# Every main product of a two-block transformer layer reads its moving operand and writes its results from the last column to the first

## The chip, the cores and the metric

The kernel runs on one core of one Trainium2 chip. The metric is device time in microseconds of one execution; the median of three runs of the kernel before is 2672.72 us (2672.32 to 2673.97).

## The reference, cut to what matters

Two transformer blocks run one after the other on a sequence of 256 positions with a model width of 2048, all in float32. Nearly all arithmetic lies in products of an activation with a weight matrix:

```python
# first block
mod = (c @ w_ada + b_ada)                      # modulation, c is one vector
h = rmsnorm(x, g_pre_mix) * (1 + scale1) + shift1
proj = h @ w_in                                # 2048 -> 9472
y_a = sliding_window_attention(...) @ w_attn_proj
y_h = (rmsnorm(hgrn2_recurrence(...)) * sigmoid(g_h)) @ w_hgrn_proj
merged = sigmoid(gate_a) * y_a + sigmoid(gate_h) * y_h
x = x + gate1 * rmsnorm(merged @ w_out, g_post_mix)
gu = h2 @ w_ffn_in                             # 2048 -> 2 x 5632
x = x + gate2 * rmsnorm((silu(g) * u) @ w_ffn_out, g_post_ffn)
# second block
proj = rms_norm(x) @ w_in_2                    # 2048 -> 4096
x = x + concat(moba_attention(q, k, v), multiscale_pool(p)) @ w_out_2
x = x + conv_ffn(rms_norm(x), w_up, conv_w, conv_b, w_down)   # 2048 -> 2 x 5632 -> 2048
```

## The kernel before

Activations lie transposed in SBUF: features on the 128 partitions, the 256 positions (`S`) along the free axis. A product with a weight matrix keeps a 128x128 piece of the weights still in TensorE and moves the activation past it; the result has output features on partitions and positions along the free axis of PSUM.

To keep float32 accuracy with TensorE's one-pass format (fp32r), every operand is split in two, a rounded part (hi) and the remainder (lo). An activation tile such as `X`, `hid`, `merged`, `attn_x` or `hgrn_x` holds for each of its 128-row blocks 512 columns: the 256 hi columns, then the 256 lo columns. For the weights, ScalarE writes `w_hi` from the raw weights (L664) and VectorE writes `w_lo` as the difference (L1174). Each 128x128 piece of weights then takes two matrix instructions, a *pair* below: `w_hi` against all 512 columns, and `w_lo` against the first 256. Both add into one PSUM bank of `psg`, 512 float32 columns wide. When a group has been summed over its contraction, ScalarE copies columns 256 to 511 to `half` (L649) and VectorE adds columns 0 to 255 to it (L1138).

The weights come in 512 KB chunks (four blocks of the contraction by 256 output columns), loaded by the SP queue into a ring of four buffers `raw`. There are 836 chunks, in twenty jobs that run one after the other (the list `jobs`, from `kv` to `dn2b`). TensorE's function `job` goes through the chunks in order: it waits for the chunk's `w_lo` (semaphore `raw_used`), issues 4 x 2 pairs, and signals `pe_chunk`. Each of the two bank numbers `b` and `b + 1` takes one of the two 128-column halves `t`, so that the order of the instructions is hi and lo into bank `b`, then hi and lo into bank `b + 1`, and again from `b` for the next block of the contraction. In the last block of a group (`kk == kt - 1`) the lo product goes first and the hi product closes the group.

Smaller products (attention, the recurrence, sums for the norms) are put between chunks by the callbacks `side` and write to `pss`. They don't go through the changed lines. All matrix instructions go through the helper `mm`, whose line is L1841, so rows with L1841 include both kinds; the tile name, `psg` or `pss`, tells them apart.

Of the kernel before, what the change touches and what calls it, by code (L numbers as in the profile page):

```python
# [17 lines left out]
S = 256  # L18
# [126 lines left out]
def two_block_kernel(nc, xT, params, cons, level_in, count_in, hot_in, rel_bias, pos, w_ada, w_in, w_attn, w_hgrn, w_out,  # L145
                     w_ffn_in, w_ffn_out, w_in2, pool_w, w_out2, w_up, w_down, out, stop_after=None):
    ctx = ExitStack()
    with ctx:
# [123 lines left out]
        psg = ctx.enter_context(nc.psum_tensor("psg", [P, 4, 512], F32))  # L272
# [121 lines left out]
        def half_slot(j, q):  # L394

            return (j.h0 + q) % RING

        def landing_of(j, i, q):

            if q >= RING:  # L400
                return landing(j, i, q - RING)
            if not is_first(i):
                return landing(j, i - 1, j.n - RING + q)
            if j.prev is None:
                return q
            return landing(j.prev, j.prev.iters - 1, j.prev.n - RING + q)

        def group_no(j, i, g):
            return j.G0 + i * len(j.groups) + g

        def bank_of(j, g):
            return 2 * ((j.G0 + g) % 2)
# [5 lines left out]
        def sums_done(j, i, g):  # L418

            return group_no(j, i, g) + 2  # L420
# [7 lines left out]
        def sum_at(j, b):  # L428

            return 13 if b < j.blocks - 1 else None  # L430
# [13 lines left out]
        def is_first(v):  # L444
            return is_static(v) and v == 0

        def turns(eng, n, body):

            body(0)
            if n == 2:  # L450
                body(1)
            elif n > 2:
                with eng.Fori(1, n) as i:
                    body(i)
# [1384 lines left out]
        def _(pe):  # L1839
            def mm(out_, l, r_, start=True, stop=True):  # L1840
                return nc.tensor.matmul(out_, l, r_, start=start, stop=stop)  # L1841

            def gate_sum(acc, b=0):

                for t in range(4):
                    o = 504 - 8 * b + 2 * t
                    ins = mm(pss[:, 3, o:o + 2], acc[:, t * P:(t + 1) * P], ones[:, 0:2])
                ins.then_inc(ada_mm, 1)

            def job(j, xs, ready=None, side=None, tile=lambda kk: kk):  # L1850

                def turn(i):
                    for p in range(j.n):
                        g, c = j.where[p]
                        b, kt, x, s = bank_of(j, g), j.groups[g][2], xs(g), half_slot(j, p)
                        if c == 0 and group_no(j, 0, g) > 0:
                            pe.wait_ge(ps_free, sums_done(j, i, g) - 2)
                        if ready and is_first(i):
                            ready(g, c)
                        pe.wait_ge(raw_used, landing_of(j, i, p) + 1)  # L1860
                        for k in range(KC):
                            kk = c * KC + k
                            at = tile((j.korder[c] if j.korder else c) * KC + k)
                            for t in range(2):
                                hi = w_hi[:, s, k, t * P:(t + 1) * P]
                                lo = w_lo[:, s, k, t * P:(t + 1) * P]
                                o = psg[:, b + t, :]
                                if kk < kt - 1:
                                    mm(o, hi, x[:, at, :], kk == 0, False)
                                    ins = mm(o[:, 0:S], lo, x[:, at, 0:S], False, False)  # L1870
                                else:
                                    mm(o[:, 0:S], lo, x[:, at, 0:S], False, False)
                                    ins = mm(o, hi, x[:, at, :], False, True)
                        ins.then_inc(pe_chunk, 1)
                        if side:
                            side(i, p)
                        if j.ada and p == 2 and (j.name == "hg" or not is_first(i)):
                            gate_block(j, i - 1, j.blocks - 1)
                        if j.name in LATE and p == 2 and is_first(i):
                            gate_block(J[LATE[j.name]], J[LATE[j.name]].iters - 1, J[LATE[j.name]].blocks - 1)  # L1880
                        for b_ in range(j.blocks):
                            if p == sum_at(j, b_):
                                gate_block(j, i, b_)

                def gate_block(j, i, b):
                    pe.wait_ge(gate_used, j.a0 + i * len(j.ada) + DT * (b + 1))
                    own = j.name == "hg" and b == 0
                    pe.wait_ge(ada_out, j.m0 + j.blocks * i + b - own)
                    gate_sum(GATES[j.name][0][i if j.name == "qa" else b], own)
                turns(pe, j.iters, turn)  # L1890
                if j.name == "out":
                    gate_block(j, j.iters - 1, j.blocks - 1)
# [90 lines left out]
            if runs("kv"):  # L1983
# [3 lines left out]
                def side(i, p):  # L1987
                    if p == 0:
                        first_terms_of(3, first_own(3)[3:])
                        first_sum(3).then_inc(ada_mm, 1)  # L1990
# [103 lines left out]
            if runs("wh"):  # L2094
                def ready(g, c):
                    if g == 0:
                        pe.wait_ge(SH["lo"], 4 * c + 4)
# [186 lines left out]
```

## Time and profile before

| | before |
|---|---|
| median of three runs | 2672.72 us |
| the profiled execution: its time | 2670.3 us |
| its span, first to last instruction | 2668.2 us |
| TensorE matmuls busy (PE) | 2550.4 us, 96% |
| TensorE weight loads busy (PEld) | 2233.3 us, 84% |
| VectorE busy (DVE) | 1833.6 us, 69% |
| ScalarE busy (ACT) | 1312.6 us, 49% |
| mean granted TensorE clock | 0.978 of full speed |
| read from HBM | 547.14 MB, 206 GB/s over the span |

PE busy counts from the start of a matmul to its modelled end. Matmuls are pipelined, so one that lasts 395 ns by the profile can be followed by the next one 235 ns after its start; the distance between two starts is the pace. The granted clock is the share of full speed that the chip gave to TensorE; full speed is 2.4 GHz and the other level, 0.50, is 1.2 GHz.

### The profile page before, as it was taken

To read this page: it belongs to the slowest core of one execution; us is meant where nothing else is said; L and a number is where in the kernel's file an instruction comes from. 1 tells how busy PE (TensorE), PEld (TensorE's weight loads), DVE (VectorE), ACT (ScalarE), POOL (GpSimd) and SP (SyncE) were. 2 spreads that over 40 slices of the span, in tenths; PEclk is the share of its full clock that TensorE was granted. 3 is DMA by queue.
4 is the path that set the end of the run, shared out by engine and by line. 5 is a ranking of instruction groups with operands and counts; after the bars stand their busy time and mean duration, and the time that the engine had idled before them with its cause. 6 is when DMAs were issued, how large, how long until landed. Compare 5 with 4: busy or idle time off the path is not lost.

```text
span 2668.2 us, 41905 instructions
## 1 busy us (share of the span) xinstructions
PE 2550.4 (96%) x14954; PEld 2233.3 (84%) x14954; DVE 1833.6 (69%) x2249; ACT 1312.6 (49%) x1693; POOL 31.1 (1%) x36
## 2 busy tenths in 40 slices
PE   4899989999997999999999989999999999999997
PEld 4888868888786888888888867888888888888886
DVE  6789997777787555676555565566677774477764
ACT  1345556566444444434444454545555554455542
POOL 0000000000000000000000000030000000000000
PEclk9699999999998999999999989999999999999999
DMA  9898974555683666798666546544555556555564
GB/s 377 306 337 305 320 266 142 165 154 158 205 293 114 189 189 189 245 304 263 189 189 190 186 137 182 174 150 150 174 176 188 190 189 197 187 175 188 190 202 134
DMA packets 491943, 550.69 MB, mean 206 GB/s; under 512 B 18776, under 2 KB 448864, under 8 KB 491840
## 3 DMA queue, kind: packets, MB, share of 16 engines
q1 hardware_dynamic: 489840, 542.10, 63.0%
q0 software_dynamic: 2000, 7.22, 0.9%
q8 instruction: 63, 1.03, 0.2%
q14 instruction: 40, 0.33, 0.0%
HBM read 547.14 MB, written 2.11 MB: 206 GB/s over the span
## 4 chain that ended last, share of the span: by engine, by line
PE 80%; DVE 9%; issue 5%; ACT 3%; DMA 1%; SPq 1%; DVEq 0%; ACTq 0%; POOL 0%
PE psg L1841 75%; PE pss L1841 5%; DVE w_lo L1174 2%; DVE gate_acc_mix L1155 2%; ACT w_hi L664 1%; DVE first_acc L1252 1%; SPq L528 1%; DMA stage<-in_w_ada 1%; DVE proj L1138 0%; DVE Pq L1389 0%; ACT X L745 0%; DVE decay L1378 0%; DVE decay L1391 0%; DVE decay L1377 0%; DMA raw<-in_w_in 0%
## 5 line engine op out<-in xcount | busy, mean ns | idle before, releaser
L1841 PE MATMUL psg<-X,w_hi 128*128 128x512 f32 x4512 | 1581.6, 395 | 21.3 <-issue 14.7
L1174 DVE TENSOR_TENSOR w_lo<-raw,w_hi 128x1024 fp32r<-128x1024 f32 x832 | 1007.8, 1229 | 633.6 <-ACT w_hi L664 625.5
L664 ACT ACTIVATE w_hi<-raw 128x1024 fp32r<-128x1024 f32 x832 | 867.0, 1057 | 834.0 <-PE psg L1841 785.0
L1841 PE MATMUL psg<-X,w_lo 128*128 128x256 f32 x4512 | 1251.0, 282 | 0.0
L1841 PEld LDWEIGHTS psg<-X,w_hi 128*128 128x128 f32 x4512 | 844.4, 189 | 198.7 <-issue 20.1
L1841 PEld LDWEIGHTS psg<-X,w_lo 128*128 128x128 f32 x4512 | 856.3, 190 | 12.2 <-issue 1.4
L1841 PE MATMUL psg<-hid,w_hi 128*128 128x512 f32 x1664 | 581.4, 394 | 0.2 <-issue 0.2
L1841 PE MATMUL psg<-hid,w_lo 128*128 128x256 f32 x1664 | 458.1, 279 | 0.0
L1841 PEld LDWEIGHTS psg<-hid,w_hi 128*128 128x128 f32 x1664 | 309.5, 187 | 71.6 <-issue 0.6
L1841 PEld LDWEIGHTS psg<-hid,w_lo 128*128 128x128 f32 x1664 | 312.0, 188 | 3.6
L649 ACT ACTIVATE half<-psg 128x512 f32<-128x512 f32 x205 | 119.0, 580 | 10.3 <-PE psg L1841 10.1
L1811 DVE SCALAR_TENSOR_TENSOR cacc<-cu,par,cacc 128x256 f32<-128x256 f32 x176 | 81.4, 483 | 49.2 <-ACT cacc L957 42.8
L1155 DVE SCALAR_TENSOR_TENSOR gate_acc_mix<-gate_w_mix,par,gate_acc_mix 128x512 f32<-128x512 f32 x150 | 112.4, 749 | 3.2
L957 ACT ACTIVATE cacc<-cu,par 128x256 f32<-128x256 f32 x88 | 48.2, 595 | 114.7 <-DVE cu L1805 114.7
L1841 PE MATMUL psg<-merged,w_hi 128*128 128x512 f32 x256 | 89.6, 395 | 0.9 <-DVE u_h L1138 0.5
L1252 DVE SCALAR_TENSOR_TENSOR first_acc<-stage,par,first_acc 128x1024 f32<-128x1024 f32 x46 | 59.1, 1284 | 16.8 <-DMA stage<-in_w_ada 15.3
L1841 PE MATMUL psg<-merged,w_lo 128*128 128x256 f32 x256 | 70.2, 279 | 0.0
L1841 PE MATMUL pss<-par,stage 128*128 128x2 f32 x224 | 41.3, 320 | 22.6 <-DMA stage<-in_w_ada 22.6
L1841 PEld LDWEIGHTS pss<-par,stage 128*128 128x128 f32 x224 | 41.2, 287 | 22.8 <-issue 11.9
L1841 PEld LDWEIGHTS psg<-merged,w_hi 128*128 128x128 f32 x256 | 47.5, 187 | 12.3 <-DVE u_h L1138 0.9
L1841 PE MATMUL psg<-hgrn_x,w_hi 128*128 128x512 f32 x128 | 45.6, 398 | 3.5 <-DVE u_h L1138 1.8
L1841 PEld LDWEIGHTS psg<-merged,w_lo 128*128 128x128 f32 x256 | 48.0, 188 | 0.7
(302 smaller groups left out, 1545.7 us busy)
## 6 DMA issues: line engine op xcount, KB each, us to landing
raw<-in_w_in SPq DMA_DIRECT2D x212, 512.0 KB, 4.5
raw<-in_w_ffn_in SPq DMA_DIRECT2D x176, 512.0 KB, 3.9
raw<-in_w_up SPq DMA_DIRECT2D x176, 512.0 KB, 5.0
raw<-in_w_ffn_out SPq DMA_DIRECT2D x88, 512.0 KB, 4.6
raw<-in_w_down SPq DMA_DIRECT2D x88, 512.0 KB, 3.4
gate_w_mix<-in_w_ada SPq DMA_DIRECT2D x160, 256.0 KB, 5.3
stage<-in_w_ada SPq DMA_DIRECT2D x64, 512.0 KB, 10.3
raw<-in_w_out SPq DMA_DIRECT2D x64, 512.0 KB, 4.5
```

Of the source, the lines that this page charges most:

```text
L528: sp.dma_start(stage[s][:, :], ada_v[:, k, m * ADA_CB:(m + 1) * ADA_CB]).then_inc(staged[s], 16)
L649: nc.scalar.activation(half[:, b // 2, :, :], psg[:, b:b + 2, CW:2 * CW], ACT.Copy).then_inc(half_ready, 1)
L664: nc.scalar.activation(w_hi[:, half_slot(j, p), :, :], raw[:, slot_of(j, p), :, :], ACT.Copy).then_inc(hi_ready, 1)
L957: nc.scalar.activation(cacc[:, g, a, :], cu[:, g, a, 2:], ACT.Identity, scale=par[:, ds(2 * i + o, 1)], bias=par[:, ds(2 * i + ob, 1)]).th ...
L1155: ins = nc.vector.scalar_tensor_tensor(acc[:, :], slots[s][:, :], ck, acc[:, :], ALU.mult, ALU.add)
L1174: nc.vector.tensor_tensor(w_lo[:, hs, :, :], raw[:, slot_of(j, p), :, :], w_hi[:, hs, :, :].bitcast(F32), ALU.subtract).then_inc(raw_used, 1)
L1252: ins = nc.vector.scalar_tensor_tensor(acc, stage[s][:, :], ck, acc, ALU.mult, ALU.add)
L1811: ins = nc.vector.scalar_tensor_tensor(cacc[:, g, a, :], cu[:, g, a, tap_:tap_ + CW], par[:, ds(2 * i + o, 1)], cacc[:, g, a, :], ALU.mult ...
L1841: return nc.tensor.matmul(out_, l, r_, start=start, stop=stop)
```

## The change

In `job` of TensorE, each of the four calls of `mm` gets its moving operand and its output with a step of -1 along the free axis. The hi product reads columns 511, 510, ..., 0 of the activation block and writes columns 511 to 0 of the bank; the lo product reads and writes columns 255 to 0. Column n of the moving operand still goes to column n of the output, the stationary operands are as they were, and so are the number of instructions, their order, all waits and all signals. No other engine's program is touched.

```diff
                                 hi = w_hi[:, s, k, t * P:(t + 1) * P]
                                 lo = w_lo[:, s, k, t * P:(t + 1) * P]
-                                o = psg[:, b + t, :]
                                 if kk < kt - 1:
-                                    mm(o, hi, x[:, at, :], kk == 0, False)
-                                    ins = mm(o[:, 0:S], lo, x[:, at, 0:S], False, False)
+                                    mm(psg[:, b + t, ::-1], hi, x[:, at, ::-1], kk == 0, False)
+                                    ins = mm(psg[:, b + t, S - 1::-1], lo, x[:, at, S - 1::-1], False, False)
                                 else:
-                                    mm(o[:, 0:S], lo, x[:, at, 0:S], False, False)
-                                    ins = mm(o, hi, x[:, at, :], False, True)
+                                    mm(psg[:, b + t, S - 1::-1], lo, x[:, at, S - 1::-1], False, False)
+                                    ins = mm(psg[:, b + t, ::-1], hi, x[:, at, ::-1], False, True)
                         ins.then_inc(pe_chunk, 1)
```

## Rows read from the trace of the kernel before

**Rows 1.** The page: busy time of each engine, and share of the span, with instruction counts.
```profile
PE 2550.4 (96%) x14954; PEld 2233.3 (84%) x14954; DVE 1833.6 (69%) x2249; ACT 1312.6 (49%) x1693; POOL 31.1 (1%) x36
```

**Rows 2.** The chain that ended last, from 1200 to 1600 us: start, length, what.
```profile
1212.82 0.79 PE pss L1841 x8
1213.60 36.46 PE psg L1841 x208
1250.06 0.79 PE pss L1841 x8
1250.85 326.16 PE psg L1841 x1872
...
1577.09 1.06 ACT w_hi L664
1578.18 1.22 DVE w_lo L1174
```

**Rows 3.** PE groups by shape: count, then busy us and mean ns, idle before.
```profile
L1841 PE MATMUL psg<-X,w_hi 128*128 128x512 f32 x4512 | 1581.6, 395 | 21.3 <-issue 14.7 <-DVE proj L1138 3.4 <-DVE w_lo L1174 2.7
L1841 PE MATMUL psg<-hid,w_hi 128*128 128x512 f32 x1664 | 581.4, 394 | 0.2 <-issue 0.2
L1841 PE MATMUL psg<-merged,w_hi 128*128 128x512 f32 x256 | 89.6, 395 | 0.9 <-DVE u_h L1138 0.5 <-DVE merged L1522 0.4
L1841 PE MATMUL psg<-attn_x,w_hi 128*128 128x512 f32 x128 | 45.9, 396 | 0.0
L1841 PE MATMUL psg<-hgrn_x,w_hi 128*128 128x512 f32 x128 | 45.6, 398 | 3.5 <-DVE u_h L1138 1.8 <-DVE hgrn_x L1423 1.7
```

**Rows 4.** PE timeline from 1500.11 us: start, length as the profile models it.
```profile
1500.11 0.39 PE L1841 MATMUL psg<-hid,w_hi 128*128 128x512 f32 x1
1500.35 0.28 PE L1841 MATMUL psg<-hid,w_lo 128*128 128x256 f32 x1
1500.46 0.39 PE L1841 MATMUL psg<-hid,w_hi 128*128 128x512 f32 x1
1500.69 0.28 PE L1841 MATMUL psg<-hid,w_lo 128*128 128x256 f32 x1
1500.81 0.39 PE L1841 MATMUL psg<-hid,w_hi 128*128 128x512 f32 x1
```

**Rows 5.** Two stretches: us, PE, PEld, DVE, ACT, POOL busy, granted clock, DMA share, GB/s.
```profile
99.01:101.57 2.56, 2.56 (x10) 2.17 (x8) 1.28 (x1) 0.54 (x1) 0.00 (x0) 0.50 1.09 384
1250.85:1577.00 326.15, 326.15 (x1872) 286.66 (x1872) 184.61 (x192) 150.51 (x171) 0.00 (x0) 1.00 0.61 188
```

**Rows 6.** PE timeline in the first of these stretches, at granted clock 0.50.
```profile
99.22 0.63 PE L1841 MATMUL psg<-X,w_hi 128*128 128x512 f32 x1
99.65 0.41 PE L1841 MATMUL psg<-X,w_lo 128*128 128x256 f32 x1
99.86 0.63 PE L1841 MATMUL psg<-X,w_hi 128*128 128x512 f32 x1
100.29 0.41 PE L1841 MATMUL psg<-X,w_lo 128*128 128x256 f32 x1
100.50 0.63 PE L1841 MATMUL psg<-X,w_hi 128*128 128x512 f32 x1
```

**Rows 7.** PE timeline at the end of a group, where lo goes before hi.
```profile
1506.18 0.39 PE L1841 MATMUL psg<-hid,w_hi 128*128 128x512 f32 x1
1506.41 0.28 PE L1841 MATMUL psg<-hid,w_lo 128*128 128x256 f32 x1
1506.53 0.63 PE L1841 MATMUL psg<-hid,w_hi 128*128 128x512 f32 x2
```

**Rows 8.** Who waited for whom, longest in total: us, times, longest.
```profile
ACT w_hi L664 <- PE psg L1841: 785.0, 497, 11.1
DVE w_lo L1174 <- ACT w_hi L664: 625.5, 448, 7.0
```

## The prediction

> **What bounds the kernel now.** I read the busy shares first. TensorE's matmuls are busy for 2550.4 of 2668.2 us, VectorE for 69% and ScalarE for 49% [rows 1]. A busy share alone doesn't say that matmuls set the end, so next comes the chain of waits. In it one piece of 326.16 us is nothing but main products, 1872 of them without a break, and where it breaks off the next steps are one split of weights on ScalarE and one on VectorE of about 1 us each [rows 2]. The wait table says the same from the other side: ScalarE's split waited 785.0 us for TensorE, and VectorE's split waited 625.5 us for ScalarE's [rows 8]. The weights are ready early; TensorE is late. Whatever the change does to the pace of a main product therefore comes out at the end one for one, and no other engine covers it.
>
> The pace has to be read from starts, not from durations. A hi product is shown as lasting 395 ns, but the lo product behind it starts 230 to 240 ns later, and the next hi product 110 to 120 ns after that [rows 4]. The long piece of the chain gives the mean: 1872 instructions are 936 pairs, and 326.16 / 936 = 348.5 ns a pair, at a granted clock of 1.00 [rows 2, 5]. A pair moves 512 + 256 = 768 columns, which at 2.4 GHz is 320.0 ns if a column goes by per cycle. So a pair has 28.5 ns over its columns. The groups by shape give the count: 4512 + 1664 + 256 + 128 + 128 = 6688 hi products, each with its lo product [rows 3], which agrees with 836 chunks of 8 pairs. Then 6688 x 348.5 ns = 2331 us of the span's 2668.2 us pass through the changed lines.
>
> **The change part by part.** It adds no instruction and removes none; it adds no wait, moves no step past any queue, and leaves the DMA bytes as they are. There are only four things that it could touch.
>
> *Reading the moving operand backwards.* No row of the kernel before shows an operand of TensorE with a step other than one, so this price isn't in the trace and has to be bounded. From below: the same 2 KB per partition are read, column by column, and neighbouring columns stay neighbours; nothing at all is the lower bound but for the rival with a gain below. [...]
>
> [...]
>
> *The order in which a PSUM column is added to again.* Before, column 0 is written by hi and again by lo 512 columns later; afterwards, column 255 is written by hi and again by lo only 256 columns later. If an addition had to wait for the one before it, this would show. But the distance of 256 exists already: at the end of a group lo comes first and hi starts over at column 0 behind it. There the start of hi follows that of lo by 0.12 us (1506.41 to 1506.53), as in the middle of a group [rows 4, 7]. I cost this at 0.
>
> *The end of a group.* ScalarE's copy and VectorE's addition wait for the whole last instruction, whichever column it ended with. They are hidden, too, since there are two sets of banks. Cost 0. The weight splits don't depend on the direction at all, and if TensorE became slower they would only wait longer.
>
> I take the lower bound, 0 ns a pair, as the likeliest. The nearer of the two rows is a judgement: the reversed stream touches the same neighbouring pairs of columns with the same start of each instruction, and differs from the full-pace row [rows 4] in one thing, the order within a pair of neighbours. It shares with the half-pace row nothing that the trace shows, since there the clock was the cause. The sum is then 0 on the profiled execution: 2668.2 us of span and 2.1 us around it, 2670.3 us. The median of the three runs is 2.4 us higher, so my forecast in their terms is 2672.7 us.
>
> [...]
>
> **The rivals.** *Half pace.* Read or write handles one column where it now handles two. For it speaks that the stream runs close to a limit: at full clock a pair needs 28.5 ns more than its columns, at half clock 0 [rows 5, 6], so something other than the array already binds a little at full speed. Against it, that the neighbours are still neighbours. The price is 640.0 - 348.5 = 291.5 ns a pair, and 6688 x 291.5 ns = 1950 us, so 2672.7 + 1950 = 4623 us. If the 28.5 ns stay on top, it is 6688 x 320 ns = 2140 us and 4813 us; if all of TensorE's idle 117.8 us (2668.2 - 2550.4) were absorbed, 4505 us. If the whole 348.5 ns doubled, 5004 us.
>
> *A small cost for each instruction.* A start at the last column might cost one period of the slower clock level more, 1 / 1.2 GHz = 0.83 ns, in each of 2 x 6688 = 13,376 instructions: 11.1 us, 2683.8 us. This decides the sign from 0.4 ns an instruction (0.2% of the time is 5.3 us). A price of ten times that, 111 us and 2784 us, would still be below anything that rows 4 could be said to exclude, since they don't show this operand.
>
> *A gain.* The 28.5 ns of a pair beyond its columns are spent somewhere in the stream. If they come from the ascending order meeting its own writes of the instruction before in the same bank, a descending order could meet them elsewhere. From 0.8 ns a pair on, it would be faster by a measurable amount; the whole 28.5 ns would be 191 us and 2482 us. Against it: the distance to the instruction before was seen to make no difference [rows 7].
>
> *The change doesn't do what it says.* The instruction as built might turn both patterns round and be the old one. Then nothing moves: 2672.7 us.
>
> **How the numbers follow.** No price: 0.50. Half pace: 0.29. A small cost for each instruction: 0.15, of which 0.01 stays within 0.2%. A gain: 0.04. No real change: 0.02. A difference of 0.2%, 5.3 us, is about what a measurement of this kernel can tell from none. Hence faster 0.04, same 0.50 + 0.01 + 0.02 = 0.53, slower 0.29 + 0.14 = 0.43. The forecast is the likeliest case's 2672.7 us, and its own range is 2667 to 2678 us. The range for 8 in 10 can't stop there, as that would leave out nearly half: it must take in half pace up to the value with 28.5 ns on top. I give 2664 to 4820 us, which leaves out the larger gains and the doubled pace. Between about 2900 and 4500 us I expect nothing; the cases are two, and the range is wide only because they are far apart.
>
> **What would show it.** Right: starts of hi and lo 235 and 115 ns apart at granted clock 1.00, 348.5 ns a pair in the long piece of the chain, and ScalarE's and VectorE's waits as they were. Half pace: 427 and 213 ns between starts with a granted clock that still reads 1.00, DMA and VectorE shares nearly halved, and waits of ScalarE for TensorE up by some 1900 us. A small cost: the same few nanoseconds on hi and on lo, where a slower stream would put twice as much on hi. The third step is wrong if lo behind hi in the middle of a group gets later while hi behind lo doesn't. The prediction as a whole falls if the stream cares which way neighbouring columns come, and that is one fact of the hardware that no row here shows.

## The result

The changed kernel takes 2689.67 us (median of 4 runs, 2687.63 to 2690.78) where the kernel before takes 2672.52 us (median of 4, 2671.43 to 2673.97): 17.2 us more, a ratio of 1.0064 with a 95% interval of 1.005 to 1.0077. It is slower, by a little and clearly. The forecast of no change was wrong, and so was the rival of half pace. The result lies in the wide range of 2664 to 4820 us, which was made to hold two cases far apart, and outside the forecast's own 2667 to 2678 us.

The page of the changed kernel, which answers to [rows 1]:

```profile
PE 2577.1 (96%) x14954; PEld 2236.6 (83%) x14954; DVE 1835.3 (68%) x2249; ACT 1314.5 (49%) x1693; POOL 31.1 (1%) x36
```

The instructions are the same in number. PE is busy 26.7 us longer, and its idle time fell from 117.8 to 111.6 us (2688.7 - 2577.1). The chain that ended last has the same long piece of main products as in [rows 2], with as many instructions in it:

```profile
1223.40 36.80 PE psg L1841 x208
1260.99 329.46 PE psg L1841 x1872
```

It took 326.16 us before and takes 329.46 us now. For 936 pairs that is 352.0 instead of 348.5 ns, so 3.53 ns more a pair. Two stretches, with the columns of [rows 5]:

```profile
99.32:101.88 2.56, 2.56 (x9) 2.18 (x8) 1.28 (x1) 0.63 (x1) 0.00 (x0) 0.50 1.09 386
1260.99:1590.45 329.46, 329.45 (x1872) 286.78 (x1872) 185.05 (x192) 150.53 (x171) 0.00 (x0) 1.00 0.61 187
```

The granted clock of the long piece is 1.00 in both kernels, so the clock isn't the cause. In the first stretch the clock was 0.50, and there the timeline shows the old pace:

```profile
99.54 0.63 PE L1841 MATMUL psg<-X,w_hi 128*128 128x512 f32 x1
99.96 0.41 PE L1841 MATMUL psg<-X,w_lo 128*128 128x256 f32 x1
100.18 0.63 PE L1841 MATMUL psg<-X,w_hi 128*128 128x512 f32 x1
...
100.82 0.63 PE L1841 MATMUL psg<-X,w_hi 128*128 128x512 f32 x1
```

That is 640 ns a pair (99.54, 100.18, 100.82), as in [rows 6]. At 0.50 that is 768 columns at 1.2 a nanosecond, which is what is meant by 1.2 GHz; 2.4 GHz is twice that, and 320.0 ns a pair is half of the 640 ns. The price was seen at a granted clock of 1.00 alone. Where in the pair it lies needs an average over the starts, which the trace holds in whole nanoseconds where the timeline prints steps of 10 ns. Over some 360 hi products and as many lo products on X from 1270 to 1400 us, hi to lo takes 233.0 ns (229.1 before) and lo to the next hi 118.1 ns (118.2 before). The pair on X went from 347.3 to 351.1 ns, and all of it is in the time that the hi product has. On `hid` it went from 350.3 to 353.3 ns. Below, "pair on X" is always such an average over about 360 pairs of this one job, good to a few tenths of a nanosecond; where another job gives another number, the text says so.

**The sum.** 6688 pairs x 3.53 ns are 23.6 us. The profile lets that be compared with the time from the first main product to the end; kernel before, then after:

```profile
98.44:2668.20 2569.76, 2494.21 (x14683) 2178.99 (x14683) 1758.33 (x2166) 1291.76 (x1662) 30.24 (x31) 0.99 0.63 199
```
```profile
98.75:2688.70 2589.95, 2518.01 (x14683) 2179.30 (x14683) 1760.08 (x2166) 1293.67 (x1662) 30.22 (x31) 0.99 0.62 198
```

TensorE is busy for 23.8 us more there, its idle time falls by 3.6 us (75.6 to 71.9), and the stretch is 20.2 us longer. (Of the 26.7 us more of busy time and the 6.2 us less of idle time over the whole span, 2.9 and 2.6 us lie in the sums ahead of the first main product, which moves by 0.3 us only.) Idle time gave something back where TensorE waits for VectorE's share of the attention and the recurrence: its waits for `probs` (L1473) went from 3.9 to 2.9 us in all, those for `r_c` (L1397) from 13.3 to 12.4 us. A stretch in which VectorE is nearly always busy, kernel before first, then after:

```profile
200.00:395.00 195.00, 183.43 (x1157) 158.27 (x1156) 187.04 (x266) 112.49 (x177) 0.00 (x0) 0.99 0.90 304
```
```profile
200.00:395.00 195.00, 188.12 (x1165) 160.28 (x1163) 184.83 (x263) 113.84 (x181) 0.00 (x0) 0.99 0.90 303
```

VectorE is busy for 187.04 of the 195 us. Of TensorE's idle time there, 11.6 and 6.9 us, the waits for `probs` are 3.9 and 2.9 us; the rest is the first part of one wait for `r_c`, which began at 387.33 us before and at 391.00 us after, lasted 11.8 and 11.6 us and runs beyond the stretch. The two profiled executions lie 20.5 us apart and the medians 17.2 us. The 3 us between are the scatter of single executions (the four of each kernel spread over about 3 us, and the profiled one of the changed kernel is its slowest), and the sum doesn't explain them.

### The profile page after: what moved, and what is told of

It is laid out like the page before. It is cut to its first block, busy times and chain, and to the rows that moved or that the text cites. A ratio compares the mean times of both kernels' runs of the same rounds, so it can differ in the third digit from the quotient of the medians.

```text
span 2688.7 us, 41905 instructions
## 1 busy us (share of the span) xinstructions
PE 2577.1 (96%) x14954; PEld 2236.6 (83%) x14954; DVE 1835.3 (68%) x2249; ACT 1314.5 (49%) x1693; POOL 31.1 (1%) x36
## 4 chain that ended last, share of the span: by engine, by line
PE 84%; DVE 7%; issue 4%; ACT 3%; DMA 1%; SPq 1%; DVEq 0%; ACTq 0%; POOL 0%
PE psg L1841 79%; PE pss L1841 5%; ACT w_hi L664 1%; DVE w_lo L1174 1%; DVE gate_acc_mix L1155 1%; DVE first_acc L1252 1%; SPq L528 1%; DMA stage<-in_w_ada 1%; DVE Pq L1389 0%; DVE proj L1138 0%; DVE decay L1391 0%; DMA raw<-in_w_in 0%; DVE decay L1377 0%; PE pss L2036 0%; DVE x L1321 0%
## 5 line engine op out<-in xcount | busy, mean ns | idle before, releaser
L1841 PE MATMUL psg<-X,w_hi 128*128 128x512 f32 x4512 | 1601.0, 401 | 20.8 <-issue 14.7
L1841 PE MATMUL psg<-hid,w_lo 128*128 128x256 f32 x1664 | 463.6, 283 | 0.0
L1252 DVE SCALAR_TENSOR_TENSOR first_acc<-stage,par,first_acc 128x1024 f32<-128x1024 f32 x46 | 59.1, 1284 | 17.2 <-DMA stage<-in_w_ada 15.7
```

Of the source, the lines that this page charges most:

```text
L1252: ins = nc.vector.scalar_tensor_tensor(acc, stage[s][:, :], ck, acc, ALU.mult, ALU.add)
```

## The experiments

All have the four calls in the form `mm(hi_o, hi, hi_x, ...)` and `mm(lo_o, lo, lo_x, ...)`, with `o = psg[:, b + t, :]` and `xi = x[:, at, :]`; each diff shows which pattern each operand has, against the kernel before. The theories: A, going down costs in itself. B, adding to a PSUM column sooner costs. C, each instruction pays for its start. D, what counts is where the reads stand to each other in SBUF.

**hi_only: the hi product goes down, lo goes up**

```diff
-hi_o, hi_x = o[:, :], xi[:, :]
+hi_o, hi_x = o[:, ::-1], xi[:, ::-1]
 lo_o, lo_x = o[:, 0:S], xi[:, 0:S]
```

> Only the hi products read and write downwards; the lo products are as before. Theory A (the stream of a hi product pays for going down, the lo product's own price is hidden since its gap is set by the next weight load): 3.5 to 4.1 ns more between the start of hi and of lo, 118 ns from lo to hi, about 2690 us as with the whole change. Theory B (the price is for adding to a PSUM column again sooner: 256 columns later where it was 512): here hi ends at column 0 and lo starts there, the distance falls to about one column, so the price is well above 4 ns and the time above 2695 us. Theory C (each instruction pays about 1.3 ns for starting at its last column): half the price, about 2681 us.

Measured: 2695.71 us, ratio 1.0097 (1.008 to 1.0114); pair on X 232.4 + 120.8 = 353.2 ns. Undoing half of the change made it dearer than the whole. C falls. A has the 3.3 ns more from hi to lo, but not the 2.6 ns more behind the lo product, which goes up as before. B, with a price well above 4 ns and over 2695 us, stays possible. (The 230.0 and 123.4 ns that a later expectation names for this run, and the 240.0 and 113.3 ns for x0_up, are averages of the timeline's rounded starts. Three pairs take 1060 ns there again and again, a whole number of the timeline's steps, so the rounding doesn't average out; the sums are right, the parts aren't.)

**lo_only: the lo product goes down, hi goes up**

```diff
 hi_o, hi_x = o[:, :], xi[:, :]
-lo_o, lo_x = o[:, 0:S], xi[:, 0:S]
+lo_o, lo_x = o[:, S - 1::-1], xi[:, S - 1::-1]
```

> Only the lo products read and write downwards. Theory A: 229.0 and 118 ns as before, 2672.5 us. Theory B: lo meets column 255 of hi 256 columns after it was written, as in the whole change, so 3.5 to 4 ns a pair, 2690 us. Theory C: half the price, 2681 us.

Measured: 2690.62 us, ratio 1.0071 (1.0055 to 1.0088); pair on X 234.6 + 116.6 = 351.2 ns, pair on `hid` 355.2 ns. A falls, as it expected nothing here: only lo goes down, and the time from hi to lo is what grows. Each half alone costs as much as both or more. A price per downward column or instruction would add up, and this doesn't.

**read_only and write_only: one side each.** Every product has its positions in reverse order in both.

```diff
# read_only
-hi_x, lo_x = xi[:, :], xi[:, 0:S]
+hi_x, lo_x = xi[:, ::-1], xi[:, S - 1::-1]
# write_only
-hi_o, lo_o = o[:, :], o[:, 0:S]
+hi_o, lo_o = o[:, ::-1], o[:, S - 1::-1]
```

> The moving operand is read downwards and the results are written upwards, in both products, so every product comes out with its positions in reverse order: the text says so, and only the time is of use. If the price lies in the reading from SBUF: 3.5 ns a pair, 2690 us. If it lies in the writing to PSUM: 2672.5 us. If it needs both, or is a mismatch of the two, something else than either.

> The moving operand is read upwards and the results are written downwards, in both products, so every product comes out with its positions in reverse order. If the price lies in the reading: 2672.5 us. If it lies in the writing: 3.5 ns a pair, 2690 us.

Measured: read_only 2692.0 us, 1.0078 (1.0061 to 1.0095); write_only 2672.55 us, 1.0002 (0.9993 to 1.0012). The long piece of the chain, read_only first:

```profile
1259.74 329.47 PE psg L1841 x1872
```
```profile
1251.87 326.16 PE psg L1841 x1872
```

Reading downwards has the whole price (329.46 us in the full change), writing downwards has none to the last digit (326.16 us in [rows 2]). In write_only a column is added to again after 256 columns, as in the full change, so B falls for that distance.

**pairs_swapped and pairs_down: order within two neighbours, or order of the pairs of neighbours.** Only the hi products differ, in operand and output alike. A "line" in the two expectations is a piece of neighbouring columns, two or more of them; no run shows how many.

```diff
# pairs_swapped: columns 1, 0, 3, 2, ...
+hi_x = xi.rearrange("p (a c) -> p a c", c=2)[:, :, ::-1]
# pairs_down: columns 510, 511, 508, 509, ...
+hi_x = xi.rearrange("p (a c) -> p a c", c=2)[:, ::-1, :]
```

> The hi products read and write columns 1, 0, 3, 2, ..., 511, 510; the lo products go upwards as before. Every two neighbours are taken in descending order, but the stream as a whole goes up and its lines come in the old order. Theory A in the form that the order within a pair of neighbours costs: 4 ns a pair or more. Theory D: 347 to 348 ns a pair, 2671.5 us. A cost for the pattern having two dimensions would show as something else.

> The hi products read and write columns 510, 511, 508, 509, ..., 0, 1; the lo products go upwards. Neighbours are ascending, the lines come downwards. Compare hi_only: 230.0 and 123.4 ns, 353.4 a pair. Theory D (lines and their order count, not the order within a line): 353 to 354 ns. If only the order within a pair counts: 347.2 ns.

Measured: pairs_swapped 2671.68 us, 0.9995 (0.9984 to 1.0007); pairs_down 2698.92 us, 1.0095 (1.0058 to 1.0131). The long pieces, in this order:

```profile
1251.33 326.17 PE psg L1841 x1872
```
```profile
1262.45 330.68 PE psg L1841 x1872
```

The first is the kernel before (326.16), the second is hi_only to the last digit:

```profile
1262.14 330.68 PE psg L1841 x1872
```

The order of two neighbours is free (326.17 against 326.16 us). What costs is the order in which the pairs of neighbours, 8 bytes each, come (330.68 us). The pattern with two dimensions of pairs_swapped costs nothing either. Two things stay open: pairs_down turns round the order of the pairs within every larger piece and the order of these pieces too, so how large a piece has to be for its order to count isn't shown; and in it, as in hi_only, lo adds again at once to the columns that hi wrote last, so a part of its 330.68 us could be B at that distance.

**x0_up, x0_down, x64_up, x64_down: the same two directions, X moved by 32 bytes.** Counted from the first weight tile, the other weight tiles begin at multiples of 2048 bytes, X at a multiple of 2048 plus 32, and `hid` and `merged` at one plus 608. A 128x128 piece of weights begins every 512 bytes. All later tiles keep their places here.

```diff
-        cursor[0] += 32
+        cursor[0] += 0        # 64 for x64
         X = place("X", [P, DT, 2 * S], R32)
-        cursor[0] += 32
+        cursor[0] += 64       # 0 for x64
```

> Every product reads and writes upwards as before; the activation tile X starts 32 bytes lower, at a multiple of 64 bytes like the weight tiles, and nothing else moves. Theory D (what a read costs depends on the addresses at which it starts and ends against those of the weight load beside it, and the kernel before sits in a cheap place): the pair on X goes from 347.2 ns to 350 ns or more with the old direction, about 2680 us, while pairs on hid stay at 350.2 ns. Theory A (going down costs in itself): 347.2 ns, 2671.5 us.

> The whole change, with X 32 bytes lower. Theory D: the pair on X changes, either way, from the 351.1 ns of the change; if the mirror image is what counts, it may fall to 347 to 349 ns. Theory A: 351.1 ns as with the change.

> Old direction. X alone starts 32 bytes higher, at a multiple of 64 bytes. If the pattern repeats every 64 bytes: as x0_up, 353.3 ns a pair (240.0 and 113.3) and 329.7 us. Otherwise something else between 347 and 355.

> The whole change, with X 32 bytes higher. If the pattern repeats every 64 bytes: as x0_down, 353.3 ns (237.4 and 115.9) and 330.8 us. If some place is as good for the downward read as 32 is for the upward one, it might be this: 347 ns, 2672 us.

Measured: x0_up 2688.45 us, 1.005 (1.0028 to 1.0073), pair on X 236.3 + 117.0 = 353.2 ns. x0_down 2695.61 us, 1.0082 (1.0053 to 1.0112), 237.7 + 115.8 = 353.5 ns. x64_up 2679.61 us, 1.003 (1.0016 to 1.0045), 230.2 + 119.0 = 349.2 ns. x64_down 2702.37 us, 1.0112 (1.0082 to 1.0141), 235.7 + 117.7 = 353.3 ns. Moving a tile by 32 bytes, with the direction as it was, costs about as much as the change under study, and at 0 the downward read costs almost nothing more than the upward one on X in this job. The pattern doesn't repeat every 64 bytes. At a granted clock of 0.50 a pair of x0_up still takes 640 ns (starts at 99.74 and 100.38), so no price of the place shows there, nor one of the direction.

**w32_x64_up and w32_x32_up: is it X's own address, or its place to the weights?**

```diff
+        cursor[0] += 32
         raw = place("raw", [P, RING, KC, CW])     # w_hi, w_lo, half behind it
...
-        cursor[0] += 32
+        cursor[0] += 32       # 0 for w32_x32
         X = place("X", [P, DT, 2 * S], R32)
-        cursor[0] += 32
+        cursor[0] += 0        # 32 for w32_x32
```

> Old direction everywhere. The weight tiles start 32 bytes higher and X 32 bytes higher too, so X is at a multiple of 64 bytes as in x0_up, but in the old position to the weights. Theory D1 (what counts is the position of the moving operand relative to the weights that are loaded beside it): 347.2 ns a pair on X and about 326.2 us in the long piece of the chain, as before. Theory D2 (what counts is X's own start against some line of the memory): 353 ns and 329.7 us, as x0_up.

> Old direction. The weight tiles start 32 bytes higher, X is where it was, so the two stand to each other as in x0_up. D1: 353 ns a pair on X. D2: 347.2 ns as before.

D1 says that X's position to the weights counts, D2 that X's own address does. Measured: w32_x64_up 2675.21 us, 1.0011 (1.0 to 1.0022), pair on X 229.0 + 118.2 = 347.2 ns. w32_x32_up 2688.97 us, 1.0066 (1.0043 to 1.0088), 236.1 + 116.9 = 353.0 ns. The query by tile shows it at a glance. Its columns are the shortest, median and longest duration of X's hi products from 1300 to 1450 us; first x0_up, then w32_x32_up, where X itself wasn't moved:

```profile
L1841 PE MATMUL psg<-X,w_hi x426: 387/398/403, 1299.6 to 1449.7; 128*128 128x512 f32 x142
```
```profile
L1842 PE MATMUL psg<-X,w_hi x426: 387/398/403, 1299.6 to 1449.7; 128*128 128x512 f32 x142
```

And the kernel before, then w32_x64_up, where both moved together:

```profile
L1841 PE MATMUL psg<-X,w_hi x433: 390/390/397, 1299.8 to 1449.8; 128*128 128x512 f32 x145
```
```profile
L1842 PE MATMUL psg<-X,w_hi x433: 390/390/397, 1299.8 to 1449.8; 128*128 128x512 f32 x145
```

In this job, two kernels with the same distance between X and the weights are twins, whatever X's own address is. D1 stands, D2 falls.

The distance isn't all that counts, though. The same products of x0_up and then w32_x32_up, from 440 to 560 us, where products on X and on `attn_x` take turns:

```profile
L1841 PE MATMUL psg<-X,w_hi x198: 389/391/580, 441.1 to 559.7; 128*128 128x512 f32 x198
```
```profile
L1842 PE MATMUL psg<-X,w_hi x196: 388/395/579, 441.7 to 559.9; 128*128 128x512 f32 x196
```

There a pair on X takes 347.0 ns in x0_up, as good as in the kernel before (346.8), and 351.1 ns in w32_x32_up. At the start of the same job as above, from 1251 to 1258 us, x0_up has 346.7 ns a pair; a group ends at 1261.5 us, and from 1264 to 1400 us it has 353.2 ns. So at distance 0 the same stream has two paces, and what came before it decides between them; no run shows by what mechanism. Over the whole kernel a pair on X takes 351.8 ns in x0_up and 353.6 ns in x0_down.

The distance between the two tiles moves a pair by up to 5.9 ns of 347 (347.3 to 353.2 ns). That speaks for reads of the moving tile and of the weights that hold each other up; but the weight tiles are also written by ScalarE and VectorE, with `raw` moved along, and no run takes these apart. In favour of the reads, x0_up's intervals from hi to lo go 241, 236, 233 ns over and over for many pairs, where ScalarE and VectorE split weights once in 8 pairs.

**x96_down, x160_down, x224_down: is there a good place for the downward read?**

```diff
-        cursor[0] += 32
+        cursor[0] += 96       # 160, 224
         X = place("X", [P, DT, 2 * S], R32)
```

All tiles behind X move up with it, by 64, 128 and 192 bytes, so `hid` comes to 160, 224 and 32 modulo 256.

> The whole change, X at 96 bytes past the weights' grid, all later tiles 64 bytes higher (hid at 672 of 2048). If going down costs in itself: 350 to 353.5 ns a pair in this place as in the three others tried (0, 32 and 64), about 2690 us. If the price is only that 32 suits the upward read: one of the new places gives 347 to 348 ns.

> The whole change, X at 160, later tiles 128 bytes higher. The same two readings as for x96_down. If the pattern repeats every 128 bytes, as with X at 32: 351.1 ns a pair.

> The whole change, X at 224, which is 32 bytes below the weights' grid of 256: the nearest to a mirror image of the old place. If a mirror image restores the pace: 347 ns a pair. If the pattern repeats every 128 bytes: as x96_down.

Measured in one run each: 2697.23, 2687.23 and 2688.42 us; pair on X 353.3, 351.1 and 351.1 ns, pair on `hid` 351.1 ns in all three. The first of the two readings holds: in none of the six places of X does the downward pair come below 351 ns. The mirror image (224) doesn't restore the pace, and the pattern doesn't repeat every 128 bytes: 96 and 224 differ.

**x32_h672_up: the rule used for a faster kernel.** X stays; the tiles behind it move up by 64 bytes, so that `hid` and `merged` are at 672 instead of 608 modulo 2048, counted from the weights.

```diff
         X = place("X", [P, DT, 2 * S], R32)
-        cursor[0] += 32
+        cursor[0] += 96
```

> Old direction, X where it was, the later tiles 64 bytes higher, so that hid and merged stand at 672 instead of 608 of 2048 (32 instead of 96 modulo 128). If the pattern repeats every 128 bytes, hid comes to the good place: its pairs go from 350.2 to 347.2 ns, and 1920 pairs x 3.0 ns give 5.8 us, about 2666 us, faster than both kernels. If it repeats every 64 bytes or depends on something else: 2672 us.

Measured: 2665.47 us against 2672.38 us, ratio 0.9976 (0.9966 to 0.9986). It is faster than both kernels, with the old direction. Over the kernel, pairs on `hid` went from 232.3 + 118.0 = 350.3 to 229.4 + 117.4 = 346.9 ns, pairs on X stayed (347.2 and 347.3 ns). The long piece:

```profile
1250.19 325.06 PE psg L1841 x1872
```

**lo384_up and lo384_down: lo products of 384 columns.** They add 128 columns of lo times lo.

```diff
-lo_o, lo_x = o[:, 0:S], xi[:, 0:S]
+lo_o, lo_x = o[:, 0:384], xi[:, 0:384]        # down: [:, 383::-1]
```

> Old direction; the lo products read and write 384 columns instead of 256 (128 columns of lo times lo are added, which the reference's products contain). 128 columns more are 53.3 ns at 2.4 GHz. If lo's 118.3 ns are set by its columns and a fixed part: 171.6 ns. If they are set by the next weight load, which needs about as long: clearly less than 171.6 ns, down to 160.

> The same with the change's direction. If the downward stream pays per column and lo was only covered by the weight load: hi 232.8 ns and lo 2.8 ns more than lo384_up has, so about 6.7 ns a pair instead of 3.9. If the price is one meeting of the two reads for each pair and not per column: 3.9 ns a pair again, at most one or two ns off.

Measured in one run each: 3016.11 and 3058.37 us. Hi to lo and lo to hi on X from 1450 to 1580 us: 229.2 and 174.8 ns upwards, 233.4 and 175.6 ns downwards. On `hid` from 1670 to 1760 us: 230.9 and 175.9, then 235.0 and 178.3 ns. The long piece, up then down:

```profile
1392.47 379.16 PE psg L1841 x1872
```
```profile
1414.44 384.25 PE psg L1841 x1872
```

Upwards, lo grew by 56.6 ns for 128 columns, not by less than 53.3, so nothing points to the next weight load as what set lo's 118.2 ns. Nor does the profile show a weight load as needing about as long: each lasts 187 to 192 ns on X in the long piece of the kernel before. The downward read costs 4.9 ns a pair on X, 6.5 ns on `hid` (2.4 of them on lo) and 5.4 ns in the long piece, where it cost 3.8, 3.0 and 3.5 ns with 256 columns. The whole kernels lie 42.3 us apart, 6.3 ns a pair. So the price grew with the columns and isn't the same once for each pair; but by how much depends on the tile and the job (X from 920 to 1200 us: 404.1 and 413.3 ns), and 6.7 ns for a price per column isn't met. The form of the price stays open.

## Why the prediction was wrong

*What bounds the kernel* was right: the pace of the pair comes out at the end nearly one for one. In the profiled executions 23.8 us more of busy time, from the first main product on, made the stretch 20.2 us longer. "One for one" was a little too strong, since 3.6 us came back from idle time.

*Reading the moving operand backwards* is the step that failed. The prediction took its lower bound, 0 ns a pair, because the reversed stream was said to differ from the full-pace row "in one thing, the order within a pair of neighbours"; the half-pace row beside it is [rows 6], with 640 ns a pair. The runs show the opposite: the order within a pair of neighbours is the one thing that is free (pairs_swapped, 326.17 us), and the order in which the pairs of neighbours come costs (pairs_down, 330.68 us). The price of the reading alone is 329.47 - 326.16 = 3.31 us in the long piece (read_only), 3.5 ns a pair, against 0 in the forecast and 291.5 ns for half pace. That the pairs come downwards was a second difference, which the prediction didn't list, and it had no term for where the tile stands to the weights.

*Writing PSUM backwards* has no term of its own in the forecast's 0. That was right: the run shows 0 for it (write_only, 326.16 us), so the price of the reading (read_only, 329.47 us) is that of the whole change (329.46 us).

*The order in which a column is added to again* at 0 was right for the distance of 256 (write_only). For the distance of one column in hi_only it wasn't isolated. The sign that the prediction gave for this step, its third, being wrong, lo behind hi later and hi behind lo not, is just what came (233.0 for 229.1 ns, 118.1 for 118.2 ns), and still the step held: reading alone gives the same two numbers (read_only). The sign didn't tell the two steps apart.

*The end of a group* at 0: the counts in the long piece and its length in write_only agree.

*The rivals.* Half pace didn't come. Its two columns for one are near the ratio of two measured paces, 640 / 348.5 = 1.84 [rows 2, 6], but the 640 ns belong to a granted clock of 0.50. No run shows the 291.5 ns more at 1.00, from which 4623 us and the upper end of the range, 4820 us, come: there the dearest average of a pair with its 768 columns was 355.2 ns (lo_only, `hid`). What was taken as a sign for it, 28.5 ns a pair beyond the columns at full clock and none at half clock, belongs to what did come: this surplus moves with the place of the tiles and with the direction, and it went from 28.5 to 32.0 ns. The small cost for each instruction had the right size within a factor of two and a bit, 0.83 ns against 1.76 ns on average, but its mechanism, a start at the last column, fell with hi_only and lo_only, where half of the downward starts cost all of the price. That the size came near was luck. The gain looked at the same surplus, with the wrong sign and a mechanism, the writes to PSUM, that write_only leaves nothing for.

**What is shown of the cause, and what isn't.** Shown: the price lies in reading the moving operand, and was seen at a granted clock of 1.00 only; the pace of a pair changes with the distance in SBUF between the moving tile and the weight tiles. The table has ns a pair at each distance modulo 256. X stands for the one job (1270 to 1400 us; 1290 to 1420 for the last three places), `hid` for the whole kernel.

| distance | up | down |
|---|---|---|
| 0 | X 353.2 | X 353.5 |
| 32 (the kernel's X) | X 347.3 | X 351.1, hid 351.1 |
| 64 | X 349.2, hid 350.6 | X 353.3 |
| 96 (the kernel's hid) | hid 350.3 | X 353.3, hid 353.3 |
| 160 | hid 346.9 | X 351.1, hid 351.1 |
| 224 | not run | X 351.1, hid 351.1 |

At four of the five distances that were run both ways the downward read costs 3 to 4 ns a pair. At 0 it costs next to nothing in this job, since the upward read is as slow there. The upward read has places that are 3 to 6 ns better than its worst, the downward read has only some that are 2 ns better, so no shift of the tiles that was tried gives the 17 us back.

The table isn't the whole rule. Downwards, X and `hid` agree wherever both were read, but the changed kernel's X took 352.6 ns from 1611 to 1800 us instead of 351.1. Upwards, X at distance 0 also ran at 347.0 ns (440 to 560 us) and X at 64 at 352.5 ns there. That the pattern repeats every 256 bytes is taken from nothing but the order of the table. That the two reads hold each other up where they come to the same part of the memory at once would fit the distances, the lost price at half clock, the jump with the direction, the growth of hi's time when only lo is turned (lo_only), and the two paces in one place. It is argued, not shown: no run took the weight load away, and none changed its direction.

## What to carry to other kernels

When a stream's pace is above its columns' time at full clock and equal to it at half clock (here 348.5 against 320.0 ns, and 640 against 640), suspect the addresses of what is read at the same time before the instruction's form, and try the tile at a few offsets of 32 bytes: here 64 bytes of padding gave 7 us. Test a rule about access order by splitting it into reading and writing and into order within and between small pieces; here writing was free (326.16 us in the long piece), and in reading the order within two neighbours was (326.17 us). Measure a pace in more than one job before making a rule of it: one place had two paces (346.7 and 353.2 ns). And don't average rounded starts of a stream that repeats in whole steps of the rounding.

## What was not expected of the hardware

- The distance of two tiles in SBUF, in steps of 32 bytes, changed TensorE's pace between 346.9 and 353.2 ns a pair with the same instructions, and the kernel between 2665.5 and 2689.0 us.
- At one and the same place a pair took 346.7 ns before a group ended and 353.2 ns after it (x0_up, 1251 to 1258 us and 1264 to 1400 us).
- Half of the change cost more than the whole: 24.2 us for hi alone and 19.1 us for lo alone (both against 2671.51 us), 17.2 us for both.
- Writing PSUM from the last column to the first cost nothing (326.16 us in the long piece both ways), nor did swapping every two neighbours of the hi products in reading and writing (326.17 us).
- At a granted clock of 0.50 a pair took 640 ns in either direction, and in x0_up too, exactly its 768 columns.
